# Keys and values change ring places, the first sampled sequence stands outside the loop, and late gate tiles are made as half the rows of two tiles

## The reference

```python
# x: (256 + 32 tokens, 2048); 8 attention heads of 128; 8 pages of 128 rows for each sampled sequence
ga, gb = h @ w_in[:, gates]                      # 2 x 2048 gate columns, each a sum over 2048 rows
k_past = cache_k[page_table]; v_past = cache_v[page_table]      # (8 sequences, 1024, 8, 128) each
R = reverse_cumsum(lf_past) - lf_past
s = concat([q @ k_past * scale + Fn + R, masked(q @ k_new * scale + Fn - Fn')])
p = softmax(s)
o_fox = p[:, :1024] @ v_past + p[:, 1024:] @ v_new
merged = sigmoid(ga) * (o_gla @ w_up_a) + sigmoid(gb) * (o_fox @ w_up_b)
x = x + gt1 * (merged @ w_out)                   # then a mixture of 16 experts, and a last norm
```

## Time and profile before

| | |
|---|---|
| median of three runs | 1856.55 us |
| the profiled execution: its time, its span | 1859.33 us, 1857.8 us |
| busy: PE, PE weight load, VectorE, ScalarE, GpSimd | 92%, 58%, 28%, 13%, 8% |
| page loads issued one by one by SyncE | 128 of 512 KB |
| late gate weights | 8 loads of 1024 KB |
| PE begins the first sampled sequence's scores | 851.3 us |
| PE ends the eighth late gate tile | 1046.1 us |

### The profile page before, as it was taken

The page is one execution under the profiler, slowest core; times in us unless marked ns, Lnnn a source line. Parts: engine busy times, 40 slices in busy tenths (PEclk is TensorE's granted clock), DMA queues, the critical chain, the costliest instruction groups (busy, mean ns, idle before and its releaser), DMA issues.

```text
span 1857.8 us, 27829 instructions
## 1 busy us (share of the span) xinstructions
PE 1717.1 (92%) x10995; PEld 1083.4 (58%) x10995; DVE 526.8 (28%) x1164; ACT 242.6 (13%) x619; POOL 153.7 (8%) x274
## 2 busy tenths in 40 slices
PE   7899999999999999996888999999689989999997
PEld 4466666666667786764666777777533333333334
DVE  3110000000018754456555121111313223332233
ACT  2010000000001200211222200000221111111113
POOL 1001111111112000240000000000010000000000
PEclk9899999999999999997999999999799999999999
DMA  9999877776624433646999795333599999999981
GB/s 338 398 382 343 301 261 295 283 274 250 247 92 152 155 104 116 229 180 225 354 392 391 293 355 206 95 148 124 211 410 426 428 428 428 428 428 427 428 359 51
DMA packets 157868, 531.13 MB, mean 286 GB/s; under 512 B 19909, under 2 KB 64107, under 8 KB 136187
## 3 DMA queue, kind: packets, MB, share of 16 engines
q1 hardware_dynamic: 128834, 432.24, 60.2%
q0 software_dynamic: 18176, 97.15, 14.0%
q10 hardware_dynamic: 10786, 0.75, 0.5%
HBM read 510.95 MB, written 19.15 MB: 285 GB/s over the span
## 4 chain that ended last, share of the span: by engine, by line
PE 66%; DMA 12%; issue 12%; SPq 3%; DVE 3%; POOL 1%; DVEq 1%; POOLq 1%; ACT 1%; ACTq 0%
PE ps L712 63%; DMA ring<-in_w_up_e_dram 6%; PE ps L722 3%; DMA xT<-in_w_ada_dram 2%; DMA xT<-in_w_in_dram 2%; DMA ring<-in_w_ada_dram 1%; SPq L437 1%; SPq L431 1%; POOL work L592 1%; POOLq L591 1%; DVE ring L1954 0%; DVE work L1571 0%; DVEq L2260 0%; DVE work L1580 0%; DMA ring<-in_cache_k_dram 0%
## 5 line engine op out<-in xcount | busy, mean ns | idle before, releaser
L712 PE MATMUL ps<-hT,ring 128*128 128x288 f32 x2304 | 586.9, 411 | 4.8 <-PE ps L712 3.3
L712 PEld LDWEIGHTS ps<-hT,ring 128*128 128x128 f32 x2304 | 430.3, 190 | 168.4 <-issue 56.8
L712 PE MATMUL ps<-ring,work 128*64 128x512 f32 (+1 forms) x1408 | 335.5, 626 | 14.6 <-DVE work L1580 6.6
L712 PE MATMUL ps<-z,ring 128*128 128x288 f32 (+1 forms) x1040 | 257.2, 409 | 4.5 <-PE ps L712 2.7
L712 PEld LDWEIGHTS ps<-z,ring 128*128 128x128 f32 x1040 | 197.5, 191 | 63.4 <-issue 6.6
L1580 DVE COPY z<-ps 128x288 f32<-128x288 f32 (+5 forms) x70 | 47.6, 686 | 535.2 <-PE ps L712 526.4
L712 PEld LDWEIGHTS ps<-ring,work 128*64 128x64 f32 (+1 forms) x1408 | 97.1, 136 | 174.0 <-issue 160.8
L1577 DVE SCALAR_TENSOR_TENSOR xT<-ps,modT,xT 128x256 f32<-128x256 f32 x144 | 63.7, 479 | 183.4 <-PE ps L712 183.3
L1363 ACT ACTIVATE z<-ps 128x512 f32<-128x512 f32 (+3 forms) x79 | 44.0, 607 | 517.0 <-PE ps L712 513.1
L1363 ACT ACTIVATE work<-ps 128x288 f32<-128x288 f32 (+2 forms) x57 | 27.7, 486 | 601.9 <-PE ps L712 601.9
L712 PE MATMUL ps<-work,z 128*128 128x288 f32 (+3 forms) x418 | 87.3, 372 | 10.8 <-DVEq L2203 7.3
(11 more groups left out here) (236 smaller groups left out, 1001.3 us busy)
## 6 DMA issues: line engine op xcount, KB each, us to landing
ring<-in_w_in_dram SPq DMA_DIRECT2D x36, 2048.0 KB, 14.2
ring<-in_w_down_e_dram SPq DMA_DIRECT2D x32, 2048.0 KB, 18.1
ring<-in_w_up_e_dram SPq DMA_DIRECT2D x24, 2048.0 KB, 19.4
ring<-in_w_ada_dram SPq DMA_DIRECT2D x16, 2048.0 KB, 16.9
z<-in_w_ada_dram POOLq DMA_DIRECT2D x32, 1024.0 KB, 7.8
xT<-in_w_ada_dram POOLq DMA_DIRECT2D x32, 1024.0 KB, 7.0
ring<-in_cache_v_dram SPq DMA_DIRECT2D x64, 512.0 KB, 5.8
ring<-in_cache_k_dram SPq DMA_DIRECT2D x64, 512.0 KB, 5.9
```

The costliest lines, as they stand in the source:

```text
L712: return nc.tensor.matmul(o, lhsT, rhs, start=start, stop=stop, skip_group_check=free)
```

## The change

Six edits go together.

1. **Places.** `KEYS, VALUES = (0, 3), (2, 1)`: the second half of the keys lies in place 3, which is free early, the second half of the values in place 1, which the last gate weights leave last. SyncE's order of places is the same, so what comes last at the start is now half the values. `up_place` swaps the second and fourth weights of the up stage to match.
2. **Peeling.** PE runs `score(0)`, `turn_probs(0)`, `late_gate(0, 0)` and then `sequence(1, 1)` ahead of its loop, which then runs three times over two sequences. The empty weighing and its bookkeeping (`lead`) go. ScalarE's and SyncE's loops also hold two sequences a turn; VectorE's is as before.
3. **Late gates.** A load brings 8 of the 16 row blocks of 256 columns, so in pieces of 1 KB where they were 512 B. Two tiles are made in banks 4 and 5. After the first half the sums go to `late_sums` in SBUF; the second half begins with a product of the identity with them. GpSimd stores both tiles at once, four times.
4. **Waits of PE.** Bank 4 also takes the last turning of `turn_probs`, so that waits for the late tile before to be copied out, and `late_gate` waits for all five copies of this sequence's probabilities.
5. **Order at the start.** PE computes the new tokens' scores before the last head is turned; VectorE turns the first quarter of the keys while PE does, masks the scores, then ends the last head. `q4` moves to ScalarE, in two parts after the exp of heads 5 and 7; `r_turn` moves to ScalarE after the last gate tile.
6. **Order of the loads.** The late weights of sequence 0 are issued before the keys of sequence 1.

```diff
-        late_w = xflat[:, 2112:2112 + KT * P].rearrange("p (k n) -> p k n", n=P)
+        late_w = xflat[:, 2112:2112 + KT * P].rearrange("p (k n) -> p k n", n=2 * P)
+        late_sums = work2[:, 2048 + T:2048 + 3 * T].rearrange("p (u t) -> p u t", u=2)
@@ SyncE
+        KEYS, VALUES = (0, 3), (2, 1)
+        def up_place(n):
+            return UP + {1: 3, 3: 1}.get(n, n)
-            def late_gate_weights(b):
-                sp.wait_ge(sem("late_gate_copied"), b + 1)
-                sp.dma_start(late_w, io["w_in"][0, :, ds(b * P + (COL_GB + 8 * P), P)]...
+            def late_gate_weights(two, half):
+                sp.wait_ge(sem("late_gate_copied"), two * 2 + (half + 1))
+                sp.dma_start(late_w, io["w_in"][0, half * 8 * P:(half + 1) * 8 * P, ds(two * 2 * P + (COL_GB + 8 * P), 2 * P)]...
             pages(0, 1)
-            pages(1, 0)
-            pages(1, 1)
             sp.wait_ge(*step("r_turn_ready"))
-            late_gate_weights(0)
-            with sp.Fori(0, DB - 2) as b:
-                pages(b + 2, 0)
-                pages(b + 2, 1)
-                late_gate_weights(b + 1)
-                pages(b + 1, 2)
-                pages(b + 1, 3)
+            late_gate_weights(0, 0)
+            pages(1, 0)
+            pages(1, 3)
+            with sp.Fori(0, DB // 2 - 1) as two:
+                for half in range(2):
+                    b = two * 2 + half
+                    pages(b + 2, 0)
+                    pages(b + 2, 3)
+                    late_gate_weights(two + half, 1 - half)
+                    pages(b + 1, 2)
+                    pages(b + 1, 1)
@@ PE
+                    if i == H_B:
+                        ... the 16 products of the new tokens' scores, from below
+                        last.then_inc(reach("s_new_ready"), 1)
                     h = i - 1
                     pe.wait_ge(sem("fox_prob"), h + 1)
@@ turn_probs
+                pe.wait_ge(sem("late_gate_copied"), b + 1)
                 for g in range(2):
                     last = tr(ps[0:TS, 4, g * P:(g + 1) * P], pE[:, g, PAST:PAST + TS])
@@ late_gate
-                for k in range(KT):
-                    last = mm(ps[:, 5, 0:T], late_w[:, k, :], hT[:, k, :], k == 0, k == KT - 1)
+                pe.wait_ge(sem("pt_copied"), b * 5 + 10)
+                for u in range(2):
+                    if half:
+                        mm(ps[:, 4 + u, 0:T], ident[:, :], late_sums[:, u, :], True, False)
+                    for k in range(8):
+                        last = mm(ps[:, 4 + u, 0:T], late_w[:, k, u * P:(u + 1) * P], hT[:, 8 * half + k, :], not half and k == 0, k == 7)
@@ the loop
-            with pe.Fori(0, DB) as b:
-                score(b)
-                weigh_values(b - 1)
-                turn_probs(b)
-                late_gate(b)
+            def sequence(b, half):
+                score(b)
+                weigh_values(b - 1)
+                turn_probs(b)
+                late_gate(b, half)
+            score(0)
+            turn_probs(0)
+            late_gate(0, 0)
+            sequence(1, 1)
+            with pe.Fori(1, DB // 2) as two:
+                for half in range(2):
+                    sequence(two * 2 + half, half)
@@ ScalarE
+                if h in (5, 7):
+                    for part in ((0, 1), (2, 3))[h // 7]:
+                        for a in range(4):
+                            last = f(q4[32 * a:32 * a + 32, :, part, :], qb[32 * part:32 * part + 32, :, TP:T], ACT.Copy)
+            act.wait_ge(*step("s_new_ready"))
+            for g in range(2):
+                last = f(r_turn[:, g, :]..., r_rep[:, g, :]..., ACT.Copy)
-                f(stage[0], ps[:, 5, 0:T], ACT.Copy).then_inc(sem("late_gate_copied"), 1)
+                f(late_sums, ps[:, 4:6, 0:T], ACT.Copy).then_inc(sem("late_gate_copied"), 1)
@@ VectorE, in the last turn of the heads
                     v.sem_inc(sem("fox_prob"), 1)
+                    if i == H_B:
+                        v.wait_ge(sem("oa_final"), 1)
+                        turn_keys(0, 0, 1, False)
                     v.wait_ge(sem("fox_turned"), h + 1)
                     copy(probT[:, h % 2, :], ps[:, 3, 0:3 * P]).then_inc(sem("fox_pt"), 1)
+                    if i == H_B:
+                        score_new()
```

More of the change, by code:

```diff
@@ L304, in freed @@
         def freed(n):
-            return place(n) + 1 + (EXTRA + lead(n % SLOTS) if n >= UP and n % SLOTS < 4 else 0)
-        def lead(s):
-            return 1 if s in (2, 3) else 0
+            return place(n) + 1 + (EXTRA if n >= UP and n % SLOTS < 4 else 0)
         def freed_for_pages(s):
-            return place(UP + s) + 1 + lead(s)
+            return place(UP + s) + 1
+        KEYS, VALUES = (0, 3), (2, 1)
+        def up_place(n):
+            return UP + {1: 3, 3: 1}.get(n, n)
         def filled(n):
@@ L1046, in _ @@
                 if i >= 1:
+                    if i == H_B:
+                        for g in range(2):
+                            for c in range(4):
+                                h = 4 * g + c
+                                o = ps[32 * c:32 * c + 32, 0, g * TS:(g + 1) * TS]
+                                mm(o, qb[:, h, TP:T], kb[:, h, TP:T], True, False)
+                                last = mm(o, ident[0:H_B, h:h + 1].to_broadcast([H_B, TS]), fT[:, TP:T], False, True)
+                        last.then_inc(reach("s_new_ready"), 1)
                     h = i - 1
@@ L1482, in sample_sequence @@
                 act.wait_ge(sem("late_gate_tile"), b + 1)
-                act.wait_ge(sem("stage_free"), b + 1)
-                f(stage[0], ps[:, 5, 0:T], ACT.Copy).then_inc(sem("late_gate_copied"), 1)
+                if not half:
+                    act.wait_ge(sem("stage_free"), two + 1)
+                f(late_sums, ps[:, 4:6, 0:T], ACT.Copy).then_inc(sem("late_gate_copied"), 1)
             act.wait_ge(sem("oa_final"), 1)
-            act.wait_ge(sem("gate_kept0"), 16 * 8)
-            with act.Fori(0, DB) as b:
-                sample_sequence(b)
+            for i in (1, 2):
+                act.wait_ge(sem(f"gate_kept{i}"), 16 * 8)
+            with act.Fori(0, DB // 2) as two:
+                for half in range(2):
+                    sample_sequence(two, half)
             for g in range(4):
@@ L1912, in _, with turn_keys, score_new @@
             v.sem_inc(reach("f_tok_copied"), 1)
+            def turn_keys(b, first=0, last=4, again=True):
+                for n in range(first, last):
+                    g, half = n // 2, n % 2
+                    if g == 0:
+                        v.wait_ge(sem(f"kv_full{KEYS[half]}"), b * 64 + 64)
+                    if again:
+                        v.wait_ge(sem("s_scored"), b * 2 + (g - 1))
+                    nc.vector.transpose(kT[:, g, 4 * half:4 * half + 4], slot(KEYS[half]).rearrange("p (n g e) -> p n g e", n=4, g=2)[:, :, g]).then_inc(sem("keys_turned"), 1)
+                    if g == 1:
+                        v.wait_ge(sem("keys_turned"), b * 4 + (n + 1))
+                        v.sem_inc(sem(f"ring_free{KEYS[half]}"), 1)
+            def score_new():
+                v.wait_ge(*step("s_new_ready"))
+                v.wait_ge(sem("kv_stored"), 6 * 16)
+                v.wait_ge(sem("state_stored"), 48)
+                tt(pS[:, :, PAST:PAST + TS], ps[:, 0, 0:2 * TS].rearrange("p (g t) -> p g t", g=2),
+                   new_mask[:, :].unsqueeze(1).to_broadcast([P, 2, TS]), ALU.add)
+                v.drain()
+                nc.vector.tensor_reduce(st_s[:, 16:18], pS[:, :, PAST:PAST + TS], AX.X, ALU.min)
+                v.drain()
+                v.sem_inc(reach("s_new_copied"), 1)
             for i in range(H_B + 1):
@@ L2002, in add_out @@
                 v.sem_inc(sem("o_all_ready"), 1)
-            turn_keys(0, 1, 4, False)
-            for g in range(2):
-                v.wait_ge(sem(f"r_rep_full{g}"), 64)
-                copy(r_turn[:, g, :].rearrange("p (a n i) -> p a n i", a=4, n=NPG), r_rep[:, g, :].rearrange("p (n a i) -> p a n i", n=NPG, a=4))
-            v.drain()
-            v.sem_inc(sem("r_turn_ready"), 1)
+            v.wait_ge(sem("r_turn_ready"), 1)
             find_max(0)
```

95 lines of the change are left out of this document (36 added, 59 removed).

## The result

The changed kernel took 1886.87 us (median of four runs, 1881.76 to 1894.75) against 1857.99 us of the kernel before: ratio 1.0163, 95% interval 1.0140 to 1.0185. It is slower by 29 us, where 13 were forecast. The profiled execution is the slowest of the four, 1894.75 us with a span of 1892.8, so its rows hold some 8 us more than the median.

The account below looks back on a forecast made before the run. Transfers were taken to set the late-gate stage's pace, with PE back to back after it. An earlier start (14.6 us) outweighed by instruction stalls put late tile 7 13.4 us later: 1859.3 becomes 1872.7, 1870 off the median; range 1841 to 1885.

Parts of the forecast that it names:

- The mechanism and its side: PE's two-sequence loop: body fetched anew each turn, PE instead of DMA sets the pace, the end comes 13.4 us later.
- Nearly double what is shown to be kept: Reason for refetching PE's loop body: nine packets, where the trace shows four and the next kept.
- Rival B: PE's two-sequence body is kept after its first turn; late tile 7 8.5 us early, 1848 us; chance 0.30.
- The stalls: PE stops at each packet of new or refetched code: 2.4 us in scores, 1.6 in weighing, 1.9 where both.
- the base of the turns: PE's own work per sequence, before stalls are added: 20.4 us in an even turn, 21.4 in an odd one.
- the falling clock: PE's clock may fall in stalls, as around a wait of 3 us (0.59); given no size.
- rival A: The forecast itself: PE's loop body refetched every turn, 1870 us, its own range 1858 to 1886; chance 0.50.
- The start: Up to late tile 0: first score at 843.8 us, tile ending at 868.0 instead of 882.6, a gain of 14.6.
- D: The start doesn't come forward because ScalarE's copies or `r_turn` are slow, with the refetching stalls: 1885 us; chance 0.05.
- C: Fetching costs PE nothing outside one stall; DMA full from 867 us, 16.5 us early, 1840 us; chance 0.15.
- the bound first given for a packet: Time from asking for an instruction packet until PE can use it: 5.0 us taken, bounds 4.4 and 6.
- Pieces and the new tiles: Late gates: 1 KB pieces lower DMA's floor from 24.0 to 23.5 us; copies' wait 1.1, identity products 1.0.

Follow-up runs that it names:

- the trace with the hint: The changed kernel with a hint of the branch back on PE's two-sequence loop: 1857.41 us, ratio 0.9998 to the kernel before.
- the kernel with only sequence 0 ahead: The changed kernel, all six edits, PE's loop body one sequence long and only sequence 0 ahead of it: 1851.11 us, ratio 0.9960.
- the short-body kernel with two sequences ahead: The changed kernel, all six edits, PE's body one sequence long by an inner loop over halves, sequences 0 and 1 ahead: 1856.85 us, ratio 1.0006.
- run 128: Not a follow-up run: "run" is a verb here, for small products that go through 128 passes in 2.6 us.

## Why the prediction was wrong

**The mechanism and its side were right.** PE's body isn't kept, nine packets come per turn, DMA falls below full, PE sets the pace. In the stage 31 packets came from 850 to 1075 us; 28 had been forecast.

**Why it isn't kept** was right in its outcome and too coarse in its reason. "Nearly double what is shown to be kept" was no argument: seven packets and one are kept, eight and one are not, eight with a hint are. The change sits on the last packet before the edge. Rival B had 0.30; with one more instruction it is what happens, at 1857 instead of 1848. In the trace with the hint late tile 3 ends at 953.8 us where B had 946.5: the start gave 2.5 of that, sequences 1 to 3, through new code, the other 4.8 (27.6, 27.1 and 28.5 us for 26.0, 24.7 and 27.8). The last four take 94.1 us, 23.5 each, just what the forecast gave the transfers, where B had 91.1 by a lead of transfers.

**The stalls** were overrated in sum. The forecast's for sequences 1 to 7, 4.6, 4.3, 6.4, 8.3, 6.4, 8.3 and 6.4, are 44.7 us in 20 stalls; the trace has 34.2 us in 16 stops of 0.15 to 3.70 (35.4 with sequence 0's). That is 10.5 us too many.

**The step that failed is the base of the turns.** "An even turn is 20.4 us of PE, an odd one 21.4", with the stalls added to it, took for granted that the passes between two stalls run at full clock. The forecast named the falling clock under rival A, gave it no size, and left it out of the sum. The scores and weighing of sequences 1 to 7 took 90.7 us without the stops, 9.5 each at full clock being 66.4: 24 us more, at a granted clock that fell to 0.50 (160 passes from 971.81 took 7.25 us). The sequence where nothing stalled, the last of the kernel with only sequence 0 ahead, took just the 21.4 of the forecast. So a term of 24 us was put at nothing, and the overrated stalls hid 10.5 of it:

| end of late tile to end of the next | predicted | measured |
|---|---|---|
| sequence 1 | 26.0 | 28.1 |
| 2 | 24.7 | 27.0 |
| 3 | 27.8 | 28.4 |
| 4, 6 (behind the jump) | 28.7 | 32.4, 33.0 |
| 5, 7 | 27.8 | 28.7, 27.5 |

Together 205.1 us for 191.5: 13.6 of the 20.3 us by which late tile 7 ended after the predicted 1059.5. Even sequences 4 and 6 exceed it most, by 3.7 and 4.3 us. Each has three stops, with two long stretches of slow passes behind them (4.51 and 7.25 us, 4.51 and 6.98).

**The start** gave the other 6.7: the first score began at 847.9, predicted 843.8, and late tile 0 ended at 874.6, predicted 868.0. In this trace gate tiles at 814 to 824 us ran at half clock (10 passes in 5.17 us, from 818.94), and everything behind moved some 4 to 5 us. To leave out what differs ahead of the stage, I count from ScalarE's copy of the same gate tile near 725 us (728.34 before, 728.16 after, 723.99 in the short-body kernel with two sequences ahead, whose gate tiles kept full clock). Tile 0 ended 154.3 us behind it before, 146.5 in the changed kernel and 141.8 in that one: the start is worth 7.8 or 12.5 us, by what one execution differs from another, where 14.6 was said. Its parts held: ScalarE's eight copies took 3.38 us (0.42 each; 0.45 was taken), its two of `r_turn` 2.00 (2.3). D has fallen.

**What the early start was worth** was overrated, where refetching doesn't cover it. C lets all of its 14.6 us pass through to the end, with transfers full from 867 us on. The kernel without the new late tiles lost nearly 8 of its 10.7 again, while DMA waited for places from 865 to 875.

**Two sums** of the forecast don't come out. C's 14.6 + 6 x 0.5 - 2.2 is 15.4, not 16.5. And the bound first given for a packet, 6 us, makes 20 us more with 20 stalls, 1890; A was priced with 5.8 instead, 1886, and the range stopped at 1885.

**Pieces and the new tiles** held: 1 KB pieces give 0.6 us a sequence where 0.5 was said. The wait for the copies was 0.81 to 0.94 us (1.1 said). The two identity products put off what follows by 1.07 us in sequence 5 (1.0 said).

## What to carry to other kernels

Count the instructions of a loop body on TensorE before making it longer: over seven packets of 256, a body is fetched anew in each turn, and a branch hint is worth one packet more. Count first runs too: peeling or writing out small products that run 128 passes in 2.6 us buys a stall at most packets, here up to 3.7 us beside full transfers. And price a stall twice, once for its length and once for the passes at half clock behind it; here the second was two thirds of the first (22 us beside 34).

## What the runs showed of the hardware

- TensorE keeps eight packets of 16 KB: 7 + 1 ahead kept (53 packets in all), 8 + 1 refetched (117), 8 with a hint kept (54), 9 with a hint refetched (119).
- A single instruction at the top of a loop moved the time by 29 us in two different kernels (1886.87 to 1857.41, 1890.12 to 1861.34).
- The packet after pass 224 of sequence 2 stopped PE for 3.13 us beside full page traffic, and 0.16 with pages cut to an eighth.
- Behind that stop of 3.13 us the same 126 passes took 6.32 us instead of 3.48; behind one of 3.70 the granted clock was 0.50, behind one of 1.20 it was 1.00.
- 193 products of one column, 386 passes, took 18.1 us, 47 ns a pass, twice what a pass of scores or weighing takes (8.91/384 = 23 ns); why wasn't looked into.
- The same gate tiles ran at full clock in some executions and at half in others (10 passes in 2.69 or 5.17 us at about 819 us), with nothing between them in the code; I know of no cause in these traces.
